# First matrix product of a fused block kernel: all eight chunks in plain fp32, small tables loaded later, norm rows sent later

## The chip, the cores and the metric

One Trainium2 chip, one core of it. The metric is device microseconds for one execution of the whole program. TensorE (PE) does the products, ScalarE (ACT) and VectorE (DVE) prepare operands and take results out of PSUM, GpSimd (POOL) helps, and SyncE (SP) issues nearly all DMAs.

## The reference, cut to what matters

The whole program computes three transformer-like blocks. The change touches only the opening of the first:

```
a0 = rmsnorm(h, norm_mix_pre[0])        # h: 272 tokens x 1024
a  = a0 @ w_dqkv                        # 1024 x (384 + 256 + 32)
c_q, c_kv, k_rope = split(a)            # c_q goes through a second rmsnorm ("cq")
```

The kernel multiplies h by the norm's gains, forms the product, and multiplies the outcome by one over the root mean square of each token afterwards. So the products don't wait for the norm; only what reads their results does.

## The kernel before, in words

Everything is kept transposed: 128 channels on the partitions, tokens along the free axis. h has eight chunks of 128 x 272. The weights come as a stream of units, and unit n uses slot n % 2 of three buffers: raw (as loaded), w_high (fp32r, the rounded part, made by ACT) and w_low (fp32r, the rest, made by DVE). The moving side is split in the same way into u_high (ACT) and u_low (DVE). A product of fp32 accuracy is then three fp32r products: high by high, high by low, low by high (the helper `three`, L519 to L521). The first units are dq (unit 0: 8 chunks x 3 blocks, for c_q), dkv (unit 1: 8 chunks x 2 blocks), dkr (unit 2: 8 chunks x 1 block), uqn (unit 3).

**The first unit is special.** Its weights go to the space of k_heads (`first_weights`) in four pieces of two chunks, each behind the two chunks of h that it meets (L382 to L385, semaphores h_in and pieces_in). Chunks 0 to 5 are multiplied as plain fp32: the stationary operand is the raw weight tile, the moving one is `first_u`, h times its gain (even chunks by ACT, L1376; odd ones by DVE, L1885). Each such product is two PE instructions in the profile, both at L812. Chunks 6 and 7 are done as `three`: ACT makes w_high of the last piece (L1385), DVE makes w_low (L1896), and only then does PE take them.

**The norm.** ACT squares each chunk into m (L1226), DVE adds the squares up in acc (L1890). Before chunk 6, PE waits for the parts of unit 0 and sums acc over the channels (`norm_sums`, L640, into bank 6). ACT takes the root (`rms`, L1243), DVE the reciprocal (L1699), and before chunk 7 PE spreads it over 128 partitions with the identity matrix (`norm_rows`, L672, into bank 7). DVE copies these rows out (`keep_rows`, L1732).

**The order of the work** is the program order of each engine, written out by hand; engines meet at semaphores. What matters around the change:

- SP: gains, the four pairs of pieces, ident (L386), dkv (L427), three small tables (par, rope, causal, L441); then dkr (L427) when the parts of unit 0 are made (`slot_free`), uqn when those of unit 1 are.
- ACT: for each piece the copy to first_u, two squares, two u_high (L1381); L1385; w_high of dkv's first half (L1205); the root (L1243); w_high of dkv's second half (L1208); a wait for the tables and ident; w_high of dkr (L1208); the squares of c_q (L1397); later the parts of uqn (L1415).
- DVE: for each piece first_u, two additions, two u_low (L1684); L1896; the reciprocal (L1699); w_low of dkv's first half (L1669); keep_rows (L1732); w_low of dkv's second half (L1675); c_q out of PSUM times the rows, three times (L1738); w_low of dkr (L1675); a wait for the tables; row_ident (L1929); the sum of c_q's squares (L1911, twice); further small steps.
- PE: chunks 0 to 5; the sums; chunk 6; the rows; chunk 7; then unit 1, whose first half needs DVE's L1669 and whose second half (chunk 4 on) needs all parts of unit 1. Before chunk 6 of unit 1 PE sums the squares of c_q (`latent_sums`, L820 and L822), for which it needs the second L1911; before chunk 7 it sends the rows of cq (L672).

Of the kernel before, what the change touches and what calls it, by code (L numbers as in the profile page):

```python
# [34 lines left out]
F32 = mybir.dt.float32  # L35
# [3 lines left out]
ALU = mybir.AluOpType  # L39
# [5 lines left out]
P = 128  # L45
D = 1024
DC = D // P
# [19 lines left out]
SCALE = float(NOPE + ROPE) ** -0.5  # L67
EPS = 1e-6

EPS_SHARE = EPS * D / P  # L70
WINDOWS = (2, 4, 8, 16)
GH, GDK, GDV = 4, 64, 128
# [21 lines left out]
FACTOR = -GUESS_A * 3.0 / 8.0  # L94


PIECES = DC // 2

# [126 lines left out]
def program(nc, dram, marks, final):  # L227
    ctx = ExitStack()
    with ctx:
# [21 lines left out]
        freed = {"v": sem("freed_v"), "a": sem("freed_a")}  # L251
        loaded = [sem("weights_loaded_0"), sem("weights_loaded_1")]
        tables_in, ident_in = sem("tables_in"), sem("ident_in")
        h_in = [sem(f"h_in_{c}") for c in range(PIECES)]
        pieces_in = [sem(f"first_unit_in_{c}") for c in range(PIECES - 1)]
        gains_in = sem("first_gains_in")
        p_in = sem("p_in")
        p_weights_in = sem("p_weights_in")
# [113 lines left out]

        def first_pieces():

            w = UNITS[0]["tiles"] * P // PIECES
            return [slice(p * w, (p + 1) * w) for p in range(PIECES)]


        @block.sync
        def _(sp):  # L380
            sp.dma_start(par[:, 0:DC], dram["par"][:, 0:DC]).then_inc(gains_in, 16)
            for p, cols in enumerate(first_pieces()):  # L382
                sp.dma_start(h[:, 2 * p:2 * p + 2, :], dram["h0"][:, 2 * p:2 * p + 2, :]).then_inc(h_in[p], 16)
                sp.dma_start(first_weights[:, cols], dram["w_dq"][0, :, cols])\
                    .then_inc(loaded[0] if p == PIECES - 1 else pieces_in[p], 16)  # L385
            sp.dma_start(ident[:, :], dram["ident"]).then_inc(ident_in, 16)  # L386

            def slot_free(n, shared=True):

# [17 lines left out]
            for name, units, tiles, _, _ in STREAM:  # L407
                n0, cols, src = FIRST_UNIT[name], tiles * P, dram["w_" + name]
                if units < 8:
                    for u in range(units):  # L410
                        n = n0 + u
                        if n == 0:
                            continue
                        if n >= 2:
                            slot_free(n, pool_share(n - 2))
                        if n == 2:
                            sp.wait_ge(loaded[0], 16)
                        dst, from_ = raw[n % 2][:, 0:cols], src[u, :, :]
                        if name == "dkr":

                            dst = dst.rearrange("p (k c) -> p k c", c=P)
                            from_ = from_.rearrange("p (k c) -> p k c", c=2 * P)[:, :, 64:64 + P]
                        if name == "uqr":

                            dst = dst.rearrange("p (k c) -> p k c", c=P)
                            from_ = from_.rearrange("p (k s c) -> p k s c", s=2, c=P)[:, :, 0, :]
                        sp.dma_start(dst, from_).then_inc(loaded[n % 2], 16)  # L427
                        if name == "uv":

                            sp.wait_ge(*done("k rope full"))  # L430
                            sp.dma_start(K[64:P, :, :], kr[64:P, :].unsqueeze(1).to_broadcast([64, NH, T1]))\
                                .then_inc(k_rope_in, 16)
                        if name == "uv":
                            q_rope_out(0)
                        if name == "wo" and u == 0:
                            for q4 in range(1, 4):
                                q_rope_out(q4)
                        if n == 1:
                            for dst, src_ in ((par[:, DC:NPAR], dram["par"][:, DC:NPAR]),
                                              (rope[:, :, :], dram["rope"]), (cmask[:, :], dram["cmask"])):  # L440
                                sp.dma_start(dst, src_).then_inc(tables_in, 16)  # L441
                else:

                    apart = 4 if pool_share(n0) != pool_share(n0 + 2) or not pool_share(n0 + 2) else 2 if not pool_share(n0 - 1) else 0
                    for u in range(apart):
                        slot_free(n0 + u, pool_share(n0 + u - 2))
                        sp.dma_start(raw[(n0 + u) % 2][:, 0:cols], src[u, :, :]).then_inc(loaded[(n0 + u) % 2], 16)
                    with sp.Fori(0, (units - apart) // 2) as i:
                        for k in range(apart, apart + 2):
                            n = 2 * i + (n0 + k)  # L450
                            slot_free(n, pool_share(n0 + k - 2))
                            sp.dma_start(raw[(n0 + k) % 2][:, 0:cols], src[2 * i + k, :, :])\
                                .then_inc(loaded[(n0 + k) % 2], 16)
# [45 lines left out]
        def _(pe):  # L499
# [292 lines left out]

            for k in range(DC):
                if k == DC - 2:
                    parts_ready(n)
                    norm_sums("a0", f"a0 acc {DC - 1}", squares(0, T1))
                if k >= DC - 2:
                    u_ready("a0")(k)
                else:
                    if k % 2 == 0:  # L800
                        pe.wait_ge(pieces_in[k // 2], 16)
                    pe.wait_ge(*done(f"a0 u {k}"))
                if k == DC - 1:
                    pe.wait_ge(ident_in, 16)
                    norm_rows("a0", token_rows(R_BANK, T1))
                for b in range(3):
                    out = bank[BLOCKS[b]["bank"]][:, 0:T1]
                    if k >= DC - 2:
                        last = three(out, *weights(n, 3 * k + b), uh[:, k, :], ul[:, k, :], False, k == DC - 1)
                    else:  # L810
                        tile = slice((3 * k + b) * P, (3 * k + b + 1) * P)
                        nc.tensor.matmul(out, first_weights[:, tile], first_u[:, k, :], start=k == 0, stop=False)  # L812
                    if k == DC - 1:
                        last.then_inc(products, 1)

            def latent_sums(name, j, what):
# [4 lines left out]
                for i, (t0, nt_) in enumerate(TILES):  # L821
                    last = nc.tensor.matmul(sums[0:nt_, i:i + 1], latent_sq[j][:, t0:t0 + nt_], over[:, what:what + 1],  # L822
                                            start=False, stop=True, skip_group_check=True)
                last.then_inc(*S.step(f"{name} sums"))
            unit(n + 1, T1, (uh, ul), u_ready("a0"), first_low="second unit low",
                 between={6: lambda: latent_sums("cq", 0, OVER_Q), 7: lambda: norm_rows("cq", latent_rows(R_BANK))})
            unit(n + 2, T1, (uh, ul))
            for k in range(QC):
                u_ready("c")(k)
# [361 lines left out]
        def _(act):  # L1191
# [177 lines left out]

            nc.scalar.activation(warm[:, :], ones[:, 0:1], ACT.Sqrt).then_inc(*S.step())  # L1370
            act.wait_ge(gains_in, 16)
            for p in range(PIECES):
                c = 2 * p
                act.wait_ge(h_in[p], 16)
                if p < PIECES - 1:
                    nc.scalar.activation(first_u[:, c, :], h[:, c, :], ACT.Copy, scale=pcol("mix_pre0", c))\  # L1376
                        .then_inc(*S.step(f"a0 u {c}"))
                for k in (c, c + 1):
                    square("a0", k, h[:, k, :], T1, S.step(f"a0 sq {k}"))
                for k in (c, c + 1):  # L1380
                    nc.scalar.activation(uh[:, k, :], h[:, k, :], ACT.Copy, scale=pcol("mix_pre0", k))\  # L1381
                        .then_inc(*S.step(f"a0 u high {k}"))
            cols = first_pieces()[PIECES - 1]
            act.wait_ge(loaded[0], 16)
            nc.scalar.activation(wh[0][:, cols], first_weights[:, cols], ACT.Copy).then_inc(high_parts, 1)  # L1385
            high(1, first="second unit", middle=lambda: rms("a0", 3))
            act.wait_ge(tables_in, 48)
            act.wait_ge(ident_in, 16)

            n = FIRST_UNIT["dq"]  # L1390
            high(n + 2)

            def latent_squares(js):
                for j in js:
# [265 lines left out]
        def _(dve):  # L1660
# [217 lines left out]
            nc.vector.memset(sq[:, :, :], 0.0).then_inc(*S.step())  # L1878
            nc.vector.memset(acc[:, :, :], EPS_SHARE).then_inc(*S.step("constants"))
            dve.wait_ge(gains_in, 16)  # L1880
            for p in range(PIECES):
                c = 2 * p + 1
                dve.wait_ge(h_in[p], 16)
                if p < PIECES - 1:
                    nc.vector.tensor_scalar(first_u[:, c, :], h[:, c, :], pcol("mix_pre0", c), None, ALU.mult)\  # L1885
                        .then_inc(*S.step(f"a0 u {c}"))
                for k in (c - 1, c):
                    dve.wait_ge(*done(f"a0 sq {k}"))
                    dve.wait_ge(*S.now())
                    nc.vector.tensor_tensor(acc[:, 0, 0:T1], acc[:, 0, 0:T1], m[:, k, :], ALU.add)\  # L1890
                        .then_inc(*S.step(f"a0 acc {k}"))
                for k in (c - 1, c):
                    u_low("a0", k, T1, 0, "mix_pre0")
            cols = first_pieces()[PIECES - 1]
            dve.wait_ge(high_parts, 1)
            nc.vector.tensor_tensor(wl[0][:, cols], first_weights[:, cols], wh[0][:, cols].bitcast(F32), ALU.subtract)\  # L1896
                .then_inc(low_parts_v, 1)
            norm("a0", tiles_of(T1))
            low(1, None, "second unit", lambda: keep_rows("a0", T1))

# [724 lines left out]
```

## Time and profile before

| | |
|---|---|
| median of 3 runs | 898.83 us (897.97 to 899.99) |
| profiled execution: span, first to last instruction | 896.4 us |
| profiled execution's own time | not listed apart from its span; the median lies 2.43 us above the span |
| PE busy | 882.7 us (98%) |
| DVE busy | 675.9 us (75%) |
| ACT busy | 503.2 us (56%) |
| POOL busy | 163.6 us (18%) |
| DMA | 146.81 MB, mean 164 GB/s |

The span runs from the first to the last instruction. Since PE is busy for nearly all of it, the page's shares tell little about a stretch of a few microseconds at the start; there the timeline of each engine is read beside that of the others. A row of the timeline has the start (us from the span's start), the duration, engine, line, operation, output and input, the count of instructions merged into it, and in brackets the idle time before it with what ended it. "SPq" is SyncE issuing a DMA.

### The profile page before, as it was taken

Reading aid. Unit: us, or ns where it says so; the run is one execution under the profiler, and the core shown is the slowest. Engines: PE = TensorE matmul, PEld = TensorE weight load, DVE = VectorE, ACT = ScalarE, POOL = GpSimd, SP = SyncE. Lnnn points to the kernel's source line nnn. Section 1 sums busy time; section 2 is a strip of 40 time slices with the busy share of each in tenths; the row PEclk is TensorE's granted clock in tenths of the full one; section 3 lists DMA queues with packets and bytes.
Section 4 is the critical chain, followed back from the end, with each engine's and each line's share of the span. In section 5 each row is a group of like instructions: output and inputs, shape, how many; then the busy total and the mean of one; then the engine's idle time right before and its main releaser. Section 6 shows DMA issues by size and latency. Waiting matters only on the chain.

```text
span 896.4 us, 19632 instructions
## 1 busy us (share of the span) xinstructions
PE 882.7 (98%) x7222; PEld 857.7 (96%) x7222; DVE 675.9 (75%) x1167; ACT 503.2 (56%) x853; POOL 163.6 (18%) x158
## 2 busy tenths in 40 slices
PE   9999999999999999999999999999999999999997
PEld 8977889999999998899999999999999999999997
DVE  7768459999994446999999544889888788875556
ACT  6777665666665347766666535554455444444443
POOL 0029530000001004200000003200032333313312
PEclk9999999999999999999999999999999999999999
DMA  7652134545455631354456454344434555564441
GB/s 251 197 126 88 58 132 158 177 181 187 167 213 184 236 152 47 107 189 182 180 187 223 168 204 158 118 166 141 141 142 171 196 188 185 186 229 176 170 141 48
DMA packets 25778, 146.81 MB, mean 164 GB/s; under 512 B 3040, under 2 KB 9216, under 8 KB 10496
## 3 DMA queue, kind: packets, MB, share of 16 engines
q1 hardware_dynamic: 25584, 145.99, 46.0%
q8 instruction: 33, 0.54, 0.3%
q14 instruction: 17, 0.14, 0.0%
q10 hardware_dynamic: 144, 0.13, 0.0%
HBM read 142.84 MB, written 1.05 MB: 161 GB/s over the span
## 4 chain that ended last, share of the span: by engine, by line
PE 94%; DVE 3%; ACT 1%; DMA 1%; issue 1%; POOL 0%; SPq 0%; DVEq 0%; POOLq 0%
PE bank L519 27%; PE bank L520 26%; PE bank L521 26%; PE bank L868 2%; PE bank L1091 1%; PE bank L884 1%; PE bank L657 1%; PE bank L672 1%; PE bank L902 1%; PE bank L640 1%; PE bank L812 1%; DMA k_heads<-w_dq_dram 1%; PE bank L1048 1%; PE bank L557 1%; PE bank L551 1%
## 5 line engine op out<-in xcount | busy, mean ns | idle before, releaser
L519 PE MATMUL bank<-u_high,w_high 128*128 128x256 f32 (+2 forms) x1318 | 376.6, 286 | 2.7 <-ACT u_high L1254 1.2
L520 PE MATMUL bank<-u_low,w_high 128*128 128x256 f32 (+2 forms) x1318 | 374.1, 284 | 0.0
L521 PE MATMUL bank<-u_high,w_low 128*128 128x256 f32 (+2 forms) x1318 | 373.0, 283 | 0.0
L519 PEld LDWEIGHTS bank<-u_high,w_high 128*128 128x128 f32 x1318 | 248.9, 189 | 5.7 <-ACT m L1226 1.7
L520 PEld LDWEIGHTS bank<-u_low,w_high 128*128 128x128 f32 x1318 | 248.6, 189 | 0.0
L521 PEld LDWEIGHTS bank<-u_high,w_low 128*128 128x128 f32 x1318 | 248.4, 188 | 0.0
L1675 DVE TENSOR_TENSOR w_low<-raw,w_high 128x1024 fp32r<-128x1024 f32 (+6 forms) x106 | 181.2, 1710 | 88.9 <-ACT w_high L1208 87.4
L1208 ACT ACTIVATE w_high<-raw 128x1024 fp32r<-128x1024 f32 (+6 forms) x115 | 179.9, 1565 | 66.8 <-PE bank L521 62.5
L519 PE MATMUL bank<-x_high,w_high 128*128 128x256 f32 (+1 forms) x592 | 167.9, 284 | 0.4 <-DVE x_low L2257 0.3
L521 PE MATMUL bank<-x_high,w_low 128*128 128x256 f32 (+1 forms) x592 | 168.2, 284 | 0.0
L520 PE MATMUL bank<-x_low,w_high 128*128 128x256 f32 (+1 forms) x592 | 167.3, 283 | 0.0
L2426 POOL TENSOR_TENSOR acc<-acc,sq 128x256 f32<-128x256 f32 (+1 forms) x32 | 44.2, 1382 | 496.4 <-ACT sq L1236 495.4
L519 PEld LDWEIGHTS bank<-x_high,w_high 128*128 128x128 f32 x592 | 111.7, 189 | 0.7 <-issue 0.7
L1205 ACT ACTIVATE w_high<-raw 128x1024 fp32r<-128x1024 f32 (+2 forms) x70 | 71.8, 1025 | 71.9 <-PE bank L521 69.7
L520 PEld LDWEIGHTS bank<-x_low,w_high 128*128 128x128 f32 x592 | 111.5, 188 | 0.0
L521 PEld LDWEIGHTS bank<-x_high,w_low 128*128 128x128 f32 x592 | 111.4, 188 | 0.0
L1669 DVE TENSOR_TENSOR w_low<-raw,w_high 128x1024 fp32r<-128x1024 f32 (+2 forms) x68 | 80.2, 1180 | 13.7 <-ACT w_high L1205 11.2
L1830 DVE SCALAR_TENSOR_TENSOR conv_out<-conv_in,par,conv_out 128x272 f32<-128x272 f32 (+1 forms) x176 | 78.9, 489 | 6.9 <-ACT conv_out L1288 1.4
L1738 DVE TENSOR_TENSOR conv_in<-bank,r_rows 128x256 f32<-128x256 f32 (+2 forms) x140 | 54.2, 427 | 16.0 <-PE bank L521 10.6
L2409 POOL TENSOR_TENSOR w_low<-raw,w_high 128x512 fp32r<-128x512 f32 (+1 forms) x22 | 46.0, 2089 | 85.9 <-ACT w_high L1208 85.9
L1295 ACT ACTIVATE conv_out<-conv_out 128x272 f32<-128x272 f32 (+1 forms) x44 | 18.7, 425 | 73.2 <-DVE conv_out L1830 73.2
L1236 ACT ACTIVATE sq<-bank 128x272 f32<-128x272 f32 (+1 forms) x24 | 9.4, 392 | 74.0 <-PE bank L521 72.1
(290 smaller groups left out, 1140.4 us busy)
## 6 DMA issues: line engine op xcount, KB each, us to landing
raw<-w_up_dram SPq DMA_DIRECT2D x66, 1024.0 KB, 4.8
raw<-w_down_dram SPq DMA_DIRECT2D x24, 1408.0 KB, 5.9
raw<-w_gin_c_dram SPq DMA_DIRECT2D x4, 1536.0 KB, 6.7
raw<-w_wo_dram SPq DMA_DIRECT2D x4, 1024.0 KB, 5.4
raw<-w_wout_dram SPq DMA_DIRECT2D x4, 1024.0 KB, 4.7
raw<-w_pgate_dram SPq DMA_DIRECT2D x4, 1024.0 KB, 4.8
raw<-w_gin_v_dram SPq DMA_DIRECT2D x2, 1024.0 KB, 4.7
raw<-w_gin_g_dram SPq DMA_DIRECT2D x2, 1024.0 KB, 5.5
```

The source lines that it names most:

```text
L519: nc.tensor.matmul(out, hi, rhi, start=start, stop=False)
L520: nc.tensor.matmul(out, hi, rlo, start=False, stop=False)
L521: return nc.tensor.matmul(out, lo, rhi, start=False, stop=stop)
L1205: nc.scalar.activation(wh[n % 2][:, 0:split], raw[n % 2][:, 0:split], ACT.Copy).then_inc(*S.step(first))
L1208: nc.scalar.activation(wh[n % 2][:, split:cols], raw[n % 2][:, split:cols], ACT.Copy).then_inc(high_parts, 1)
L1295: nc.scalar.activation(cv[:, 0, 0:T], cv[:, 0, 0:T], ACT.Silu).then_inc(*S.step(f"silu {l} {k}"))
L1669: nc.vector.tensor_tensor(wl[n % 2][:, 0:split], raw[n % 2][:, 0:split], wh[n % 2][:, 0:split].bitcast(F32), ALU.subtract)\
L1675: nc.vector.tensor_tensor(wl[n % 2][:, split:cols], raw[n % 2][:, split:cols], wh[n % 2][:, split:cols].bitcast(F32), ALU.subtract).then_i ...
L1738: nc.vector.tensor_tensor(out, bank[BLOCKS[b]["bank"]][:, 0:T], rows[:, 0:T], ALU.mult)\
L1830: nc.vector.scalar_tensor_tensor(cv[:, hf, 0:T], ur[:, hf, skip + tap:skip + tap + T], pcol(f"cw{l}", (tap * 2 + hf) * FC + j), cv[:, hf, ...
L2409: nc.gpsimd.tensor_tensor(wl[n % 2][:, at], raw[n % 2][:, at], wh[n % 2][:, at].bitcast(F32), ALU.subtract).then_inc(low_parts_g, pool_cou ...
L2426: nc.gpsimd.tensor_tensor(acc[:, a, 0:T], acc[:, a, 0:T], x, ALU.add).then_inc(*step)
```

## The change

It does four things. The list of pieces becomes a tuple of chunk pairs. Chunks 6 and 7 of unit 0 are multiplied as plain fp32 like the others: the split of the last piece's weights (L1385, L1896) is dropped, and the copies to first_u of chunks 6 (ACT) and 7 (DVE) come in. The norm's sums go from before chunk 6 to before chunk 7, its rows from before chunk 7 of unit 0 to before chunk 1 of unit 1. And SP issues ident after dkv, behind a new wait until dkv has landed, and the three tables behind ident; ACT's wait for the tables and ident goes behind its w_high of dkr.

```diff
+BY_SCALAR = (0, 2, 4, 6)
-PIECES = DC // 2
+PIECES = tuple((c, c + 1) for c in range(0, DC, 2))
...
         @block.sync
...
-                    .then_inc(loaded[0] if p == PIECES - 1 else pieces_in[p], 16)
-            sp.dma_start(ident[:, :], dram["ident"]).then_inc(ident_in, 16)
+                    .then_inc(loaded[0] if p == len(PIECES) - 1 else pieces_in[p], 16)
...
                         if n == 1:
+                            sp.wait_ge(loaded[1], 16)
+                            sp.dma_start(ident[:, :], dram["ident"]).then_inc(ident_in, 16)
                             for dst, src_ in ((par[:, DC:NPAR], dram["par"][:, DC:NPAR]),
                                               (rope[:, :, :], dram["rope"]), (cmask[:, :], dram["cmask"])):
                                 sp.dma_start(dst, src_).then_inc(tables_in, 16)
...
         @block.tensor
...
             for k in range(DC):
                 if k == DC - 2:
+                    pe.wait_ge(loaded[0], 16)
                     parts_ready(n)
-                    norm_sums("a0", f"a0 acc {DC - 1}", squares(0, T1))
-                if k >= DC - 2:
-                    u_ready("a0")(k)
-                else:
-                    if k % 2 == 0:
-                        pe.wait_ge(pieces_in[k // 2], 16)
+                for p, chunks in enumerate(PIECES[:-1]):
+                    if k == chunks[0]:
+                        pe.wait_ge(pieces_in[p], 16)
+                if k < DC - 2:
                     pe.wait_ge(*done(f"a0 u {k}"))
                 if k == DC - 1:
-                    pe.wait_ge(ident_in, 16)
-                    norm_rows("a0", token_rows(R_BANK, T1))
+                    norm_sums("a0", f"a0 acc {DC - 1}", squares(0, T1))
                 for b in range(3):
                     out = bank[BLOCKS[b]["bank"]][:, 0:T1]
-                    if k >= DC - 2:
-                        last = three(out, *weights(n, 3 * k + b), uh[:, k, :], ul[:, k, :], False, k == DC - 1)
-                    else:
-                        tile = slice((3 * k + b) * P, (3 * k + b + 1) * P)
-                        nc.tensor.matmul(out, first_weights[:, tile], first_u[:, k, :], start=k == 0, stop=False)
+                    tile = slice((3 * k + b) * P, (3 * k + b + 1) * P)
+                    last = nc.tensor.matmul(out, first_weights[:, tile], first_u[:, k, :], start=k == 0, stop=k == DC - 1)
...
+            def first_rows():
+                pe.wait_ge(ident_in, 16)
+                norm_rows("a0", token_rows(R_BANK, T1))
             unit(n + 1, T1, (uh, ul), u_ready("a0"), first_low="second unit low",
-                 between={6: lambda: latent_sums("cq", 0, OVER_Q), 7: lambda: norm_rows("cq", latent_rows(R_BANK))})
+                 between={1: first_rows, 6: lambda: latent_sums("cq", 0, OVER_Q), 7: lambda: norm_rows("cq", latent_rows(R_BANK))})
...
         @block.scalar
...
-                if p < PIECES - 1:
-                    nc.scalar.activation(first_u[:, c, :], h[:, c, :], ACT.Copy, scale=pcol("mix_pre0", c))\
-                        .then_inc(*S.step(f"a0 u {c}"))
+                for c in chunks:
+                    if c in BY_SCALAR:
+                        nc.scalar.activation(first_u[:, c, :], h[:, c, :], ACT.Copy, scale=pcol("mix_pre0", c))\
+                            .then_inc(*(S.step(f"a0 u {c}") if c < DC - 2 else (high_parts, 1)))
...
-            cols = first_pieces()[PIECES - 1]
-            act.wait_ge(loaded[0], 16)
-            nc.scalar.activation(wh[0][:, cols], first_weights[:, cols], ACT.Copy).then_inc(high_parts, 1)
             high(1, first="second unit", middle=lambda: rms("a0", 3))
+
+            n = FIRST_UNIT["dq"]
+            high(n + 2)
             act.wait_ge(tables_in, 48)
             act.wait_ge(ident_in, 16)
-
-            n = FIRST_UNIT["dq"]
-            high(n + 2)
...
         @block.vector
...
-                if p < PIECES - 1:
-                    nc.vector.tensor_scalar(first_u[:, c, :], h[:, c, :], pcol("mix_pre0", c), None, ALU.mult)\
-                        .then_inc(*S.step(f"a0 u {c}"))
+                for c in chunks:
+                    if c not in BY_SCALAR:
+                        nc.vector.tensor_scalar(first_u[:, c, :], h[:, c, :], pcol("mix_pre0", c), None, ALU.mult)\
+                            .then_inc(*(S.step(f"a0 u {c}") if c < DC - 2 else (low_parts_v, 1)))
...
-            cols = first_pieces()[PIECES - 1]
-            dve.wait_ge(high_parts, 1)
-            nc.vector.tensor_tensor(wl[0][:, cols], first_weights[:, cols], wh[0][:, cols].bitcast(F32), ALU.subtract)\
-                .then_inc(low_parts_v, 1)
             norm("a0", tiles_of(T1))
             low(1, None, "second unit", lambda: keep_rows("a0", T1))
```

## Rows read from the trace of the kernel before

**Rows 1.** The page, part 1: busy time, share of the span, instructions.
```profile
PE 882.7 (98%) x7222; PEld 857.7 (96%) x7222; DVE 675.9 (75%) x1167; ACT 503.2 (56%) x853; POOL 163.6 (18%) x158
```
**Rows 2.** PE's waits, whole span, longest total: us in total, times, longest.
```profile
PE bank L519 <- ACT u_high L1254: 1.2, 2, 1.0
```
**Rows 3.** The chain that ended last, in order of time: start, us, what.
```profile
8.41 5.77 PE bank L812 x24
14.18 0.49 issue
14.67 0.61 PE bank L640 x6
...
16.54 0.64 PE bank L672 x6
```
**Rows 4.** Timeline of PE around the norm's rows and unit 1.
```profile
16.38 0.80 PE L672 MATMUL bank<-ident,norm_y 91*128 91x91 f32 x6
...
18.18 0.29 PE L519 MATMUL bank<-u_high,w_high 128*128 128x272 f32 x1
...
22.71 0.35 PE L820 MATMUL bank<-ones,eps_weights 128*128 128x3 f32 x2
```
**Rows 5.** Timeline of ACT, 12 to 27 us.
```profile
12.43 0.83 ACT L1385 ACTIVATE w_high<-k_heads 128x768 fp32r<-128x768 f32 x1
14.47 1.06 ACT L1205 ACTIVATE w_high<-raw 128x1024 fp32r<-128x1024 f32 x1 [1.21 <-DMA raw<-w_dkv_dram]
15.43 0.15 ACT L1243 ACTIVATE norm_t<-bank 91x3 f32<-91x3 f32 x1
...
19.02 1.06 ACT L1208 ACTIVATE w_high<-raw 128x1024 fp32r<-128x1024 f32 x1 [2.48 <-DMA raw<-w_dkr_dram]
...
26.81 0.51 ACT L1415 ACTIVATE w_high<-raw 128x384 fp32r<-128x384 f32 x1
```
**Rows 6.** Timeline of DVE, 11 to 23 us.
```profile
11.89 0.99 DVE L1890 TENSOR_TENSOR acc<-acc,m 128x272 f32<-128x272 f32 x2
...
13.62 0.95 DVE L1896 TENSOR_TENSOR w_low<-k_heads,w_high 128x768 fp32r<-128x768 f32 x1
15.61 0.17 DVE L1699 RECIPROCAL norm_y<-norm_t 91x3 f32<-91x3 f32 x1 [1.04 <-ACT norm_t L1243]
15.71 1.19 DVE L1669 TENSOR_TENSOR w_low<-raw,w_high 128x1024 fp32r<-128x1024 f32 x1
17.21 0.44 DVE L1732 COPY r_rows<-bank 128x272 f32<-128x272 f32 x1 [0.32 <-PE bank L672]
17.69 1.22 DVE L1675 TENSOR_TENSOR w_low<-raw,w_high 128x1024 fp32r<-128x1024 f32 x1
18.83 1.13 DVE L1738 TENSOR_TENSOR m<-bank,r_rows 128x272 f32<-128x272 f32 x3
20.11 1.23 DVE L1675 TENSOR_TENSOR w_low<-raw,w_high 128x1024 fp32r<-128x1024 f32 x1
...
22.12 0.44 DVE L1911 TENSOR_TENSOR sq<-sq,m 128x272 f32<-128x272 f32 x1
```
**Rows 7.** Timeline of SP: DMA issues of the tables and of dkr.
```profile
5.01 0.65 SPq L386 DMA_DIRECT2D ident<-ident_dram  x1
...
7.65 0.47 SPq L441 DMA_DIRECT2D causal<-cmask_dram  x1
14.65 0.67 SPq L427 DMA_DIRECT2D raw<-w_dkr_dram  x1
```
**Rows 8.** DMA issues up to 60 us: count, KB each, median us to landing.
```profile
raw<-w_uqn_dram SPq DMA_DIRECT2D x1, 1536.0 KB, 6.9
...
raw<-w_dkr_dram SPq DMA_DIRECT2D x1, 512.0 KB, 4.2
...
ident<-ident_dram SPq DMA_DIRECT2D x1, 64.0 KB, 6.8
...
par<-par_dram SPq DMA_DIRECT2D x1, 4.0 KB, 1.7
```

More of the change, by code:

```diff
@@ L253, in program @@
         tables_in, ident_in = sem("tables_in"), sem("ident_in")
-        h_in = [sem(f"h_in_{c}") for c in range(PIECES)]
-        pieces_in = [sem(f"first_unit_in_{c}") for c in range(PIECES - 1)]
+        h_in = [sem(f"h_in_{c}") for c in range(len(PIECES))]
+        pieces_in = [sem(f"first_unit_in_{c}") for c in range(len(PIECES) - 1)]
         gains_in = sem("first_gains_in")
@@ L373, in first_pieces @@
         def first_pieces():
-            w = UNITS[0]["tiles"] * P // PIECES
-            return [slice(p * w, (p + 1) * w) for p in range(PIECES)]
+            w = UNITS[0]["tiles"] * P // DC
+            return [(slice(cs[0], cs[-1] + 1), slice(cs[0] * w, (cs[-1] + 1) * w)) for cs in PIECES]
         @block.sync
@@ L381, in _ @@
             sp.dma_start(par[:, 0:DC], dram["par"][:, 0:DC]).then_inc(gains_in, 16)
-            for p, cols in enumerate(first_pieces()):
-                sp.dma_start(h[:, 2 * p:2 * p + 2, :], dram["h0"][:, 2 * p:2 * p + 2, :]).then_inc(h_in[p], 16)
+            for p, (chunks, cols) in enumerate(first_pieces()):
+                sp.dma_start(h[:, chunks, :], dram["h0"][:, chunks, :]).then_inc(h_in[p], 16)
                 sp.dma_start(first_weights[:, cols], dram["w_dq"][0, :, cols])\
-                    .then_inc(loaded[0] if p == PIECES - 1 else pieces_in[p], 16)
-            sp.dma_start(ident[:, :], dram["ident"]).then_inc(ident_in, 16)
+                    .then_inc(loaded[0] if p == len(PIECES) - 1 else pieces_in[p], 16)
             def slot_free(n, shared=True):
@@ L1371, in _ @@
             act.wait_ge(gains_in, 16)
-            for p in range(PIECES):
-                c = 2 * p
+            for p, chunks in enumerate(PIECES):
                 act.wait_ge(h_in[p], 16)
-                if p < PIECES - 1:
-                    nc.scalar.activation(first_u[:, c, :], h[:, c, :], ACT.Copy, scale=pcol("mix_pre0", c))\
-                        .then_inc(*S.step(f"a0 u {c}"))
-                for k in (c, c + 1):
+                for c in chunks:
+                    if c in BY_SCALAR:
+                        nc.scalar.activation(first_u[:, c, :], h[:, c, :], ACT.Copy, scale=pcol("mix_pre0", c))\
+                            .then_inc(*(S.step(f"a0 u {c}") if c < DC - 2 else (high_parts, 1)))
+                for k in chunks:
                     square("a0", k, h[:, k, :], T1, S.step(f"a0 sq {k}"))
-                for k in (c, c + 1):
+                for k in chunks:
                     nc.scalar.activation(uh[:, k, :], h[:, k, :], ACT.Copy, scale=pcol("mix_pre0", k))\
                         .then_inc(*S.step(f"a0 u high {k}"))
-            cols = first_pieces()[PIECES - 1]
-            act.wait_ge(loaded[0], 16)
-            nc.scalar.activation(wh[0][:, cols], first_weights[:, cols], ACT.Copy).then_inc(high_parts, 1)
             high(1, first="second unit", middle=lambda: rms("a0", 3))
+            n = FIRST_UNIT["dq"]
+            high(n + 2)
             act.wait_ge(tables_in, 48)
             act.wait_ge(ident_in, 16)
-            n = FIRST_UNIT["dq"]
-            high(n + 2)
             def latent_squares(js):
@@ L1880, in _ @@
             dve.wait_ge(gains_in, 16)
-            for p in range(PIECES):
-                c = 2 * p + 1
+            for p, chunks in enumerate(PIECES):
                 dve.wait_ge(h_in[p], 16)
-                if p < PIECES - 1:
-                    nc.vector.tensor_scalar(first_u[:, c, :], h[:, c, :], pcol("mix_pre0", c), None, ALU.mult)\
-                        .then_inc(*S.step(f"a0 u {c}"))
-                for k in (c - 1, c):
+                for c in chunks:
+                    if c not in BY_SCALAR:
+                        nc.vector.tensor_scalar(first_u[:, c, :], h[:, c, :], pcol("mix_pre0", c), None, ALU.mult)\
+                            .then_inc(*(S.step(f"a0 u {c}") if c < DC - 2 else (low_parts_v, 1)))
+                for k in chunks:
                     dve.wait_ge(*done(f"a0 sq {k}"))
@@ L1891, in _ @@
                         .then_inc(*S.step(f"a0 acc {k}"))
-                for k in (c - 1, c):
+                for k in chunks:
                     u_low("a0", k, T1, 0, "mix_pre0")
-            cols = first_pieces()[PIECES - 1]
-            dve.wait_ge(high_parts, 1)
-            nc.vector.tensor_tensor(wl[0][:, cols], first_weights[:, cols], wh[0][:, cols].bitcast(F32), ALU.subtract)\
-                .then_inc(low_parts_v, 1)
             norm("a0", tiles_of(T1))
```

## Prediction

> **What bounds the kernel now.** I read the page first: PE is busy for 882.7 us of 896.4 [rows 1], so what counts is PE's order of work and its few gaps. Then the list of PE's waits: the largest entry is 1.2 us in total, and every entry is ended by an engine or by "issue", none by a DMA [rows 2]. So a delay at the start has nothing later to dissolve in: the transfers run ahead of PE, and what PE does wait for (DVE, ACT) works on PE's own results and shifts with it. Then the chain of waits around the edit: 24 passes of plain fp32 from 8.41 to 14.18, a gap of 0.49, the norm's sums (0.61), then chunk 6, the rows (0.64), chunk 7 [rows 3]; unit 1 begins at 18.18, and the sums of c_q's squares at 22.71 [rows 4]. Last the timelines of ACT, DVE and SP beside it [rows 5 to 7]. The thing to see is in DVE's: from 15.71 on it works almost without a break, and its last step before 22.71, the second L1911, ends at 22.12 + 0.44 = 22.56 [rows 6], while PE gets to the sums that need it at 22.71. DVE feeds PE with no slack worth the name at that point.
>
> **First unit, PE.** A plain product is two passes of 5.77 / 24 = 0.240 us [rows 3], 0.481 together. Three fp32r products take 3 x 0.126 = 0.378: 36 of them lie between 18.18 and 22.71 [rows 4]. Chunks 6 and 7 (six tiles) go from 6 x 0.378 = 2.27 to 6 x 0.481 = 2.89, so 0.62 more. The gap of 0.49 goes: it ends with DVE's w_low of the last piece (13.62 + 0.95 = 14.57 [rows 6]), which is no longer made. The rows leave this unit (-0.64) and return in unit 1 (+0.64). On paper PE is at 14.18 + 1.44 = 15.62 with chunk 6, 16.23 with the sums, 17.67 with chunk 7, and free of unit 0 half a microsecond earlier than 18.18.
>
> Here a rule speaks against the edit. The row shows 0.481 for an fp32 product [rows 3]. The Trainium skill, FP8 and Floating Point Precision, section TensorE Precision Notes, has true fp32 as four passes through the array. With the pass spacing of 0.126 that would be 0.504 as an estimate, so chunk 6 would end 0.07 later and everything behind it too. The measured 0.481 is used.
>
> **Covers of the first unit.** ACT's copy for chunk 6 and DVE's for chunk 7 come in, but L1385 (0.83) and L1896 (0.95) go [rows 5, 6]; both engines end no later. The last weight piece had landed by 12.43, when ACT read it without waiting [rows 5], and acc is complete at 11.89 + 0.99 = 12.88 [rows 6], about 13.4 with the added copies. PE needs them at 14.18 and 15.62: nothing. If this cover were gone, each microsecond of lateness would go straight to PE.
>
> **Unit 1, first half.** The sums now start at 15.62 instead of 14.67, 0.95 later. DVE takes the reciprocal before w_low of dkv's first half, in program order. Before, L1669 started at 15.71, 1.04 behind the start of the sums, and ended at 16.90 [rows 3, 6]. Now it ends at 15.62 + 2.23 = 17.85, and with 0.10 for the signal (14.57 to 14.67 in rows 3 and 6) PE starts unit 1 at 17.95, having waited 0.28. dkv itself is no limit: it came at 14.47 [rows 5], and with fewer transfers around it, no later.
>
> **The rows, and what is queued behind them.** This is the term that decides. PE sends the rows after chunk 0 of unit 1: 17.95 + 6 x 0.126 + 0.08 for the restart = 18.79, against 16.38 before [rows 4]. DVE's keep_rows followed 0.83 behind (17.21 [rows 6]), so now at 19.62, 2.41 later. Behind keep_rows DVE has, in this order: w_low of dkv's second half, c_q out of PSUM, w_low of dkr, row_ident, the two sums of squares. From 17.21 to 22.56 that is 5.35 us, and only 0.15 of it is idle (19.96 to 20.11, a wait for ACT's w_high of dkr) [rows 6]. So now it ends at 19.62 + 5.20 = 24.82, and PE can start the sums of cq at about 24.9. PE itself would be there at 17.95 + 0.08 + 36 x 0.126 + 0.64 = 23.2, so it stalls for 1.7 us before chunk 6 of unit 1. Chunk 4 is not held up: the second half of w_low is ready at 19.62 + 0.48 + 1.22 = 21.3, PE asks for it at 21.7. Against 22.71 PE is **2.2 us late** there. From there on the order of all engines is as before.
>
> **Tables, ident, dkr.** SP now waits for dkv to land (14.4 at the latest, from 14.47 in rows 5; perhaps 13.5, as 0.6 MB no longer share the engines), then issues ident and three tables, each 0.5 to 0.7 us [rows 7], then dkr. So dkr is issued at 16.1 to 17.0 instead of 14.65. It took 4.2 us [rows 8]; behind the tables perhaps half a microsecond more. It lands between 20.3 and 21.7, ACT has its w_high 1.1 later [rows 5], at 21.4 to 22.8. DVE comes to it at 22.3 (keep_rows at 19.62, plus 2.75 to the end of L1738 in rows 6). So 0 in the middle of the range, up to 0.5 at its end, more if the transfer is slower still. ident, issued about 14, needs between 1.7 (4 KB, empty queue) and 6.8 (behind all the weights) [rows 8]; I take near 2, as the queue is empty then. It is needed at 18.8, so nothing; at the far end it would add 2. The tables are read by DVE after 23.5. uqn is issued when w_low of unit 1 is done, now 21.4, takes 6.9 [rows 8] and lands at 28.3; ACT read it at 26.81 [rows 5], shifted to 29.0: 0.7 to spare. POOL only clears acc after the norm's sums, a microsecond later, and has nothing due; its queue isn't touched otherwise. ACT's wait for tables moves behind a wait (dkr) that ended later anyway.
>
> **The sum.** +2.2 on the profiled execution: 896.4 to 898.6 for the span. The median shown, 898.83, is 2.43 above that span; I carry this over: 901.0.
>
> **The rivals.**
> 1. dkr late. SP's wait puts dkr behind four issues. It decides once dkr lands after 21.2; each microsecond beyond goes to PE one for one, as low(dkr) stands before the squares in DVE's queue. A further microsecond, or ident near its far bound, gives 902.0. For it: dkr took 4.2 us for 512 KB in a quiet stretch, so it is a slow transfer. Against: the tables are nearly through when it starts.
> 2. Not slower: DVE's queue has room that the timeline hides. If the squares are there before PE at 23.2, that is, if what lies behind keep_rows can be done in 3.5 us and not in 5.2, only PE's own sum is left: 17.95 + 0.64 - 18.18 = +0.4, so 899.2. For it: a DVE late here could catch up if PE's later steps asked less of it, and a wait in the attention part could take some of it back. Against: the rows show no idle time to draw on, and PE's waits are short and none is for a DMA.
> 3. The edit does its plain job: PE free 0.5 us earlier and the rows slip into a hole. 898.3. For it: the gap of 0.49 does go. Against: 0.62 more product time, and PE has no hole in unit 1.
>
> **Chances.** Forecast (900.3 to 901.7) 0.58; rival 1 0.15; rival 2 0.20; rival 3 0.07. A measurement of this kernel can tell 0.2% from no change, 1.8 us: slower means above 900.6. A fifth of the forecast's own case lies below that (sums rounded my way, run spread of about 1 us), so slower 0.58 x 0.8 + 0.15 = 0.61, faster 0.04, same 0.35. Range 899.0 to 902.6: it leaves out rival 3 and the far tail of rival 1.
>
> **What would show it.** In the changed profile: L812-like passes without a gap from 8.41 to about 15.6, sums there, unit 1 from about 17.95, L672 at 18.8, keep_rows at 19.6, PE's L820 near 24.9 with an idle time of 1.5 to 1.9 us before it, released by DVE's L1911, and every stage from 25 us on shifted by about 2.2. Rival 1: ACT's w_high of dkr starts after 21.2 and DVE idles before its w_low. Rival 2: L820 at about 23.2. I am wrong if PE shows no wait before L820, or if the shift at 25 us isn't there at the end.

## The result, and the profile after

The changed kernel takes 901.37 us in the median of 5 runs (900.21 to 903.05), against 898.83 (897.83 to 899.99, 5 runs) before. The two medians are 2.5 us apart; the ratio is 1.0035, 95% interval 1.0024 to 1.0046, which is about 3.1 us slower. The spans of the two profiled executions, 899.5 and 896.4 us, are 3.1 us apart as well. The prediction said slower, by 2.2; the time lies in its range, but a good third of the loss came in a way that it did not have.

The changed profile, page part 1, and the longest entry of PE's waits:

```profile
PE 884.9 (98%) x7216; PEld 859.4 (96%) x7216; DVE 675.1 (75%) x1167; ACT 503.0 (56%) x853; POOL 163.6 (18%) x158
```
```profile
PE bank L818 <- DVE pool_gains L1925: 1.6, 1, 1.6
```

PE has one new wait, 1.65 us long (the list cuts it to 1.6), and it is now the longest of the program ([rows 2] had 1.2 in two). The timeline of PE shows where it is. Line numbers have moved: L810 is the plain fp32 product, L643 the norm's sums, L675 the rows, L818 and L820 the sums of c_q's squares.

```profile
15.34 0.57 PE L643 MATMUL bank<-mean_weights,acc 128*91 128x1 f32 x6
15.77 1.62 PE L810 MATMUL bank<-q_heads,k_heads 128*128 128x272 f32 x6
...
17.48 0.40 PE L522 MATMUL bank<-u_high,w_high 128*128 128x272 f32 x1
...
18.35 0.80 PE L675 MATMUL bank<-ident,norm_y 91*128 91x91 f32 x6
...
22.65 0.28 PE L524 MATMUL bank<-u_high,w_low 128*128 128x272 f32 x1
24.59 0.35 PE L818 MATMUL bank<-ones,eps_weights 128*128 128x3 f32 x2 [1.65 <-DVE pool_gains L1925]
24.80 0.72 PE L820 MATMUL bank<-mean_weights,sq 128*128 128x1 f32 x6
...
26.67 1.29 PE L675 MATMUL bank<-ident,norm_y 128*128 128x128 f32 x6
```

Unit 1 starts at 17.48, 0.7 earlier than before (18.18 in [rows 4]). Nearly all of that, 0.64 us, is the norm's rows, which PE has yet to send and now sends inside unit 1. Its last product before cq's sums starts at 22.65, so without the wait PE would have been at the sums at about 22.8, against 22.71 before: in PE's own work the edit gains nothing. The norm's rows are 2.0 later (18.35 against 16.38), and the sums of cq start at 24.59 instead of 22.71, **1.88 later**, behind 1.65 us in which PE does nothing. The releaser is named as DVE's pool_gains; it is the step beside the second sum of squares, which is what PE's wait asks for. DVE's timeline has the whole queue of [rows 6] again, shifted:

```profile
16.24 1.19 DVE L1667 TENSOR_TENSOR w_low<-raw,w_high 128x1024 fp32r<-128x1024 f32 x1
19.18 0.44 DVE L1730 COPY r_rows<-bank 128x272 f32<-128x272 f32 x1 [1.75 <-PE bank L675]
19.66 1.23 DVE L1673 TENSOR_TENSOR w_low<-raw,w_high 128x1024 fp32r<-128x1024 f32 x1
20.81 1.13 DVE L1736 TENSOR_TENSOR m<-bank,r_rows 128x272 f32<-128x272 f32 x3
21.99 1.23 DVE L1673 TENSOR_TENSOR w_low<-raw,w_high 128x1024 fp32r<-128x1024 f32 x1
...
24.00 0.44 DVE L1905 TENSOR_TENSOR sq<-sq,m 128x272 f32<-128x272 f32 x1
```

DVE stands idle for 1.75 us in front of keep_rows (0.32 before), and then needs 24.44 - 19.18 = 5.26 us to the end of the squares, as it did before (5.35). The second suspect, dkr, is close by. ACT's timeline, and SP's:

```profile
20.89 1.06 ACT L1209 ACTIVATE w_high<-raw 128x1024 fp32r<-128x1024 f32 x1 [3.83 <-DMA raw<-w_dkr_dram]
```
```profile
14.10 0.33 SPq L441 DMA_DIRECT2D ident<-ident_dram  x1
...
15.98 0.67 SPq L428 DMA_DIRECT2D raw<-w_dkr_dram  x1
```

dkr is issued 1.3 later and lands at 20.9 instead of 19.0. Its w_high ends at 21.95, and DVE begins w_low of dkr at 21.99, when it has just finished L1736 (21.94). Two limits end within 0.05 us of each other. The profile's chain that ended last goes through dkr here and has the late rows (18.35) nowhere:

```profile
15.98 4.88 DMA raw<-w_dkr_dram
20.89 1.07 ACT w_high L1209
```

A chain follows only the releaser that came last. Whether the other would have held as long has to be tried (runs 1 to 3).

The sums start 1.88 late, but the end is 3.1 late. The rest shows in the windows (busy time and count of PE, PEld, DVE, ACT, POOL; then granted clock as a share of 2.4 GHz, DMA share, GB/s), first after, then before:

```profile
20.00:25.00 5.00, 3.35 (x28) 3.16 (x27) 4.60 (x10) 2.02 (x4) 0.00 (x0) 1.00 0.60 189
25.00:30.00 5.00, 5.00 (x30) 4.96 (x30) 3.23 (x9) 1.55 (x5) 0.00 (x0) 0.66 0.88 289
26.00:27.00 1.00, 1.00 (x6) 1.00 (x6) 0.94 (x3) 0.00 (x0) 0.00 (x0) 0.50 0.89 326
30.00:35.00 5.00, 5.00 (x42) 5.00 (x41) 4.77 (x8) 5.00 (x9) 0.00 (x0) 1.00 0.01 2
```
```profile
25.00:30.00 5.00, 4.96 (x40) 4.77 (x39) 4.52 (x10) 3.95 (x7) 0.00 (x0) 1.00 0.50 136
```

From 25 to 30 us PE is busy throughout and gets 30 instructions done instead of 40: **the granted clock fell from 2.4 to 1.2 GHz** for some three microseconds behind the wait. The products there start 0.23 us apart (25.99 and 26.22) instead of 0.126:

```profile
25.99 0.43 PE L522 MATMUL bank<-u_high,w_high 128*128 128x272 f32 x1
26.22 0.43 PE L523 MATMUL bank<-u_low,w_high 128*128 128x272 f32 x1
```

What that costs shows in PE's next landmark, the first product of uqn, after and then before:

```profile
32.31 0.29 PE L522 MATMUL bank<-latent_high,w_high 128*128 128x272 f32 x1
```
```profile
29.08 0.36 PE L519 MATMUL bank<-latent_high,w_high 128*128 128x272 f32 x1
```

From the start of cq's sums to this product PE takes 7.72 us instead of 6.37, so the delay has grown from 1.88 to 3.23 there, and 3.1 is left of it at the end. So 3.1 = 1.88 (late squares) + 1.2 (lower clock). The Trainium skill (TensorE: Matmul & The Clock Gate, section HAM oscillation) says that idle gaps of PE bring the throttled clock back. The trace agrees in kind, 0.66 in the window behind the gap, but the page's rule speaks of longer gaps than the 1.65 us here; the measurement decides. What PE did before the clock fell: 1.65 us of nothing, then the short sums with one to three columns, then the first two products at full pace (25.45 and 25.68).

### The profile page after: what moved, and what is told of

It is laid out like the page before. It is cut to its first block, busy times and chain, and to the rows that moved or that the text cites. A ratio compares the mean times of both kernels' runs of the same rounds, so it can differ in the third digit from the quotient of the medians.

```text
span 899.5 us, 19618 instructions
## 1 busy us (share of the span) xinstructions
PE 884.9 (98%) x7216; PEld 859.4 (96%) x7216; DVE 675.1 (75%) x1167; ACT 503.0 (56%) x853; POOL 163.6 (18%) x158
## 3 DMA queue, kind: packets, MB, share of 16 engines
HBM read 142.84 MB, written 1.05 MB: 160 GB/s over the span
## 4 chain that ended last, share of the span: by engine, by line
PE 92%; DVE 3%; DMA 2%; ACT 1%; issue 1%; SPq 1%; POOL 0%; DVEq 0%; POOLq 0%
PE bank L522 26%; PE bank L523 26%; PE bank L524 26%; PE bank L869 2%; PE bank L1092 1%; DMA raw<-w_dkv_dram 1%; PE bank L885 1%; PE bank L660 1%; PE bank L675 1%; PE bank L903 1%; PE bank L643 1%; PE bank L1049 1%; PE bank L560 1%; PE bank L554 1%; PE bank L995 1%
## 5 line engine op out<-in xcount | busy, mean ns | idle before, releaser
L1736 DVE TENSOR_TENSOR conv_in<-bank,r_rows 128x256 f32<-128x256 f32 (+2 forms) x140 | 54.2, 427 | 16.1 <-PE bank L524 10.7
```

What stands on the lines that cost most here:

```text
L1736: nc.vector.tensor_tensor(out, bank[BLOCKS[b]["bank"]][:, 0:T], rows[:, 0:T], ALU.mult)\
```

## The experiments

Ten kernels ran, each timed in five rounds beside the kernel before on the same chip (its medians there 898.21 to 898.32 us). "Start of cq's sums" is 22.71 in the kernel before. The expectations name two theories of what holds DVE's queue: A, the late rows alone; B, the rows and dkr together.

**1. Rows right after unit 0.** The changed kernel with:

```diff
+            first_rows()
             unit(n + 1, T1, (uh, ul), u_ready("a0"), first_low="second unit low",
-                 between={1: first_rows, 6: ...
+                 between={6: ...
```

> The changed kernel, but the norm's rows are sent right after unit 0, ahead of the wait for unit 1, about 0.95 us earlier. Theory A (only the late rows delay DVE's queue): DVE is 0.9 earlier throughout, the sums of cq start at 23.7 instead of 24.6, the end is at least 0.9 us earlier. Theory B (dkr, issued behind ident and the tables, is a second limit that lies right behind the first: ACT's w_high of dkr started at 20.89 and DVE's w_low at 21.99): DVE's keep_rows comes 0.9 earlier but its w_low of dkr still starts at 22.0, the sums of cq stay at 24.6, and the time stays at +3 us over the kernel before.

Measured: 901.17 us, ratio 1.0033 (1.0020 to 1.0045): nothing gained. DVE and PE in its profile:

```profile
18.31 0.44 DVE L1731 COPY r_rows<-bank 128x272 f32<-128x272 f32 x1 [0.64 <-PE bank L675]
...
21.87 1.23 DVE L1674 TENSOR_TENSOR w_low<-raw,w_high 128x1024 fp32r<-128x1024 f32 x1 [0.81 <-ACT w_high L1210]
```
```profile
24.47 0.35 PE L818 MATMUL bank<-ones,eps_weights 128*128 128x3 f32 x2 [1.65 <-DVE pool_gains L1926]
```

keep_rows comes 0.9 earlier, and DVE loses it again in a wait of 0.81 for dkr's w_high, which wasn't there. That is theory B. The shown execution took 903.96 us, the other five 900.86 to 901.21; why it was longer is taken up at the end.

**2. Tables early, as before.** The changed kernel with:

```diff
+            sp.dma_start(ident[:, :], dram["ident"]).then_inc(ident_in, 16)
...
-                            sp.wait_ge(loaded[1], 16)
-                            sp.dma_start(ident[:, :], dram["ident"]).then_inc(ident_in, 16)
```

> The changed kernel, but SP issues ident ahead of dkv and the tables right behind dkv, without the wait, as before the change. Theory B (rows and dkr limit together): dkr's w_high is ready long before, but DVE still comes to w_low of dkr at 21.94 instead of 21.99, because the rows are as late; no change, +3 us. Rival (SP's order alone makes the loss): the sums of cq start 1 to 1.9 us earlier.

Measured: 901.28 us, ratio 1.0037 (1.0025 to 1.0049): nothing gained either. ACT has dkr's w_high at 17.17, nearly four microseconds earlier, and the sums of cq start at 24.12, 9.1 behind the norm's sums (15.02), as in the changed kernel (9.25). The rows now hold alone. ACT and PE in its profile:

```profile
17.17 1.06 ACT L1208 ACTIVATE w_high<-raw 128x1024 fp32r<-128x1024 f32 x1 [0.43 <-DMA raw<-w_dkr_dram]
```
```profile
24.12 0.36 PE L817 MATMUL bank<-ones,eps_weights 128*128 128x3 f32 x2 [1.52 <-DVE pool_gains L1924]
```

**3. Both.** (The first and the third run that the expectation names are runs 1 and 2 here.)

> The edits of the first and the third run of this call together: rows right after unit 0 and tables issued early. Theory B: only both together help. DVE comes to w_low of dkr at about 21.0, the sums of cq start at 23.5, PE waits some 0.8 us, the granted clock stays at 1.00, and the end is 0.8 us over the kernel before. Theory A: the same as the first run. If the clock falls here too, 2 us over.

Measured: 899.18 us, ratio 1.0012 (1.0003 to 1.0021), the start of cq's sums at 23.57:

```profile
23.57 0.35 PE L817 MATMUL bank<-ones,eps_weights 128*128 128x3 f32 x2 [0.74 <-DVE pool_gains L1925]
```

Each alone is worth nothing; together 2.0 of the 2.9 us by which run 1 lay above the same kernel before come back: 0.9 in DVE's queue (24.47 in run 1, 23.57 here), the rest with the clock, which stayed at 1.00 in this profile and fell in one execution of eleven. This is what two limits with the same end look like.

**4. DVE's order changed.** The changed kernel with c_q's squares added before the w_low of dkr:

```diff
             latents_in(range(QC))
+            add_latent_squares((1, 2))
             low(2)
+            norm("cq", 3)
...
-            add_latent_squares((1, 2))
...
-            norm("cq", 3)
```

> The changed kernel, but DVE adds c_q's squares before its w_low of dkr and takes cq's reciprocal right behind it. Theory: the stall is DVE's program order. The sums of cq then start near 23.7 (limited by ACT, which squares after its w_high of dkr), PE waits 0.8 us instead of 1.65, TensorE's granted clock stays at 1.00, and the end is 1.0 us over the kernel before instead of 3.1. Rival: the loss is in the fp32 products or in the DMA order, then nothing changes and it stays at +3.

Measured: 899.91 us, ratio 1.0018 (1.0009 to 1.0027), the sums at 23.27 behind a wait of 0.52.

```profile
23.27 0.35 PE L818 MATMUL bank<-ones,eps_weights 128*128 128x3 f32 x2 [0.52 <-DVE sq L1905]
...
30.18 0.36 PE L522 MATMUL bank<-latent_high,w_high 128*128 128x272 f32 x1 [0.58 <-DVE w_low L1948]
```

Rows, tables and products are as in the changed kernel; moving two additions, and cq's reciprocal behind them, takes 1.3 us off (against the 901.2 of runs 1 and 2). The sums came earlier than expected, and yet the end is 1.6 over the kernel before instead of 1.0. A wait of 0.58 for the first w_low of uqn comes up at 30.18, where the kernel before goes on almost without one: what DVE does earlier for one consumer it does later for the next.

**5. One part alone.** The kernel before, with nothing but the rows moved into unit 1.

> The kernel before with one part of the change: the norm's rows go from before chunk 7 of unit 0 to before chunk 1 of unit 1; products, tables and sums as before. Theory (the rows are the culprit): rows at 18.3, keep_rows at 19.1, the sums of cq at 24.4 to 24.5 instead of 22.7, PE waits 1.7 us there. With the clock falling behind that wait +3 us at the end, without it +1.7. Rival (it takes the fp32 products or the tables): within 0.5 us of the kernel before.

Measured: 899.99 us, ratio 1.0023 (1.0013 to 1.0033).

```profile
18.41 0.80 PE L672 MATMUL bank<-ident,norm_y 91*128 91x91 f32 x6
...
24.50 0.35 PE L817 MATMUL bank<-ones,eps_weights 128*128 128x3 f32 x2 [1.51 <-DVE pool_gains L1931]
```
```profile
25.00:30.00 5.00, 5.00 (x42) 4.96 (x42) 3.77 (x10) 2.33 (x6) 0.00 (x0) 1.00 0.90 297
```

The rows alone make the whole delay: 24.50, 1.79 late. In the profiled execution the clock stayed at 1.00 and the span is 898.1, 1.7 over the kernel before. The nine executions fall into two groups: five at a mean granted clock of 0.998 (899.63 to 899.99) and four at 0.996 or 0.997 (900.89 to 901.50). The same wait is followed by the fall in one execution and not in the next (by the mean clock, as only one execution has a profile), and the fall costs 1.3 us.

**6. The wait filled with work.** The changed kernel with eleven spare products in front of cq's sums:

```diff
             def latent_sums(name, j, what):
+                if name == "cq":
+                    for _ in range(11):
+                        nc.tensor.matmul(bank[5][:, 0:T1], wh[1][:, 0:P], uh[:, 0, :], start=True, stop=True)
                 pe.wait_ge(*done(f"latent squares {j}"))
```

> The changed kernel with 11 spare fp32r products of 128 x 272 (into a bank nobody reads) in front of the sums of cq, 1.4 us of work where PE waited 1.65. They compute nothing that is used. Theory C (the idle time makes the clock fall, and that costs 1.2 us on top): the sums still start at 24.6, the granted clock stays at 1.00 in 25 to 30, and the end is 1.2 us earlier than in the changed kernel, +1.9 over the kernel before. Rival (the clock is not tied to this gap): still 0.66 in 25 to 30 and +3.1.

Measured: 899.89 us, ratio 1.0018 (1.0009 to 1.0028); 0.998 or 0.999 in all eleven executions. The sums start at 24.68, no earlier than in the changed kernel, and PE is busy all along:

```profile
23.08 1.55 PE L818 MATMUL bank<-u_high,w_high 128*128 128x272 f32 x11
24.68 0.38 PE L821 MATMUL bank<-ones,eps_weights 128*128 128x3 f32 x2
```
```profile
25.00:30.00 5.00, 5.00 (x43) 4.96 (x43) 3.61 (x11) 2.13 (x6) 0.00 (x0) 1.00 0.94 311
```

Useless work in the gap makes the kernel about 1.5 us faster (1.0018 against 1.0035, each to the kernel before, timed beside it). From the sums to the first product of uqn PE takes 6.39 us again (24.68 to 31.07), where it took 7.72 with the fallen clock. That is the clock's part by itself. The changed kernel wasn't timed beside this one, but runs 5 and 7 were, and there the clock fell in 11 of 19 executions behind waits of 1.51 and 0.89 us; here it fell in none of 11. So the idle time was its cause.

**7 and 8. Dose.** The kernel before with three, and with one, useless copies on DVE ahead of the squares:

```diff
+            for _ in range(3):
+                dve.wait_ge(*S.now())
+                nc.vector.tensor_copy(xf[:, :], rows[:, :]).then_inc(*S.step())
             add_latent_squares((1, 2))
```

> The kernel before with three useless DVE copies (128 x 272, in a chain, 0.55 us each) ahead of the sums of c_q's squares. Theory: DVE has no slack there, so PE waits 1.6 us before the sums of cq, and nothing later takes it back: +1.6 at the end, and +2.8 if the clock falls behind the wait. Rival (later waits take it up): under +0.5.

> The same with one such copy, 0.55 us. Theory: PE waits 0.5 us, the granted clock stays at 1.00, +0.5 at the end: the clock part comes only with the long wait. Rival: the clock falls here too, +1.7. If later waits take it up: 0.

Measured: 900.33 us, ratio 1.0021 (1.0011 to 1.0030), and 898.81, ratio 1.0003 (0.9994 to 1.0012). A chained copy took 0.36 us, not 0.55 (the three 1.08, from 21.54 to 22.62), so the waits are 0.9 and 0.3:

```profile
23.76 0.35 PE L820 MATMUL bank<-ones,eps_weights 128*128 128x3 f32 x2 [0.89 <-DVE pool_gains L1934]
```
```profile
23.56 0.36 PE L820 MATMUL bank<-ones,eps_weights 128*128 128x3 f32 x2 [0.31 <-DVE pool_gains L1934]
```

With three copies the sums are 1.05 late and the profiled span, 897.3, is 0.9 over 896.4: nearly nothing of the delay is taken back later. With one copy the difference is within the noise, though its profile has the wait. In this second profile the norm's sums were themselves 0.4 late (15.11), so its 23.56 isn't the copy alone. With three copies, seven of ten executions ran at 0.996 or 0.997, with a median of 900.53, against 899.36 for the other three: again 1.2 us.

**9. Everything repaired.** Edits 1, 2 and 4 together.

> The changed kernel with rows right after unit 0, tables issued early, and DVE adding c_q's squares before its w_low of dkr (cq's reciprocal right behind it). Theory: no wait of PE before the sums of cq, which start at about 22.6; granted clock 1.00; the end within 0.3 us of the kernel before, rather below it. If the products in fp32 cost more than they look, up to +0.5.

Measured: 898.46 us against 898.32, ratio 1.0009 (0.9999 to 1.0019). The sums start at 22.54, 0.17 ahead of the kernel before, without a wait. It is lost at once: DVE is later for uqn.

```profile
29.37 0.36 PE L521 MATMUL bank<-latent_high,w_high 128*128 128x272 f32 x1 [0.58 <-DVE w_low L1948]
```

The kernel before restarts there at 29.08. One execution of the twelve took 903.48 at a mean clock of 0.997; what happened in it isn't known.

**10. The fp32 products alone.** The kernel before with chunks 6 and 7 in plain fp32, sums before chunk 6, rows before chunk 7, tables early.

> The kernel before with one part of the change: chunks 6 and 7 in plain fp32, the split of the last weight piece dropped; sums before chunk 6, rows before chunk 7, tables early, as before. Theory: 0.62 us more product time against the gap of 0.49 and what the first pieces give; unit 1 starts between 17.9 and 18.3 against 18.18, and the end is within 0.3 us of the kernel before. Rival (the fp32 products are a loss or a gain by themselves): more than 0.5 us either way.

Measured: 898.17 us against 898.32, ratio 0.9997 (0.9989 to 1.0006). The gap of 0.49 is gone and the longer products eat it.

```profile
14.57 0.57 PE L642 MATMUL bank<-mean_weights,acc 128*91 128x1 f32 x6
...
23.12 0.28 PE L819 MATMUL bank<-ones,eps_weights 128*128 128x3 f32 x2
```

From the end of chunk 5 to cq's sums it is 8.55 us (14.57 to 23.12), against 8.53 before (14.18 to 22.71). The expected start of unit 1 was missed in this profile (18.40), since PE was through chunk 5 and at the norm's sums only at 14.57, without a gap, where 14.18 had been taken. No version clearly beats the kernel before.

How often the clock fell, with PE's wait before cq's sums in each kernel's one profile:

| kernel | wait, us | executions with mean clock 0.997 or less |
|---|---|---|
| rows after unit 0 (1) | 1.65 | 6 of 6 |
| changed | 1.65 | 4 of 5 |
| tables early (2) | 1.52 | 6 of 6 |
| only rows moved (5) | 1.51 | 4 of 9 |
| three copies (7) | 0.89 | 7 of 10 |
| rows and tables (3) | 0.74 | 1 of 11 |
| squares first (4) | 0.52 | 0 of 11 |
| one copy (8) | 0.31 | 0 of 11 |
| wait filled (6) | none | 0 of 11 |
| everything repaired (9) | none (0.58 later, at 29.37) | 1 of 12 |
| fp32 products alone (10) | none | 0 of 11 |

## Why the prediction was right or wrong

**The deciding term held.** The prediction put the loss in DVE's queue behind keep_rows: 5.20 us from there to the end of the squares, 5.26 measured; PE 2.2 late at cq's sums behind a wait of 1.7, measured 1.88 and 1.65. Run 5 shows it with the rows alone, run 7 that there is no slack at the point: three copies of 1.08 us together made the sums 1.05 late.

**The first unit** came out earlier than its sum. The pass cost (0.240) was right, but the prediction took over the arrival at 14.18 from the profile of before, and with it two small losses that the changed execution did not have: a first product at 5.30 instead of 5.18, and some 0.2 us between the end of chunk 1 (12 passes from 5.30, so 8.18) and 8.41, where the second piece starts. The norm's sums started at 15.34, not 15.62. ACT, now idle, took the root 0.60 behind them and not 0.76. So unit 1 began at 17.48, not 17.95, without the wait of 0.28. That is more than the difference between 2.2 and 1.88. DVE gave 0.05 of it back at dkr, for which it was ready at 21.94 and which it began at 21.99.

**Tables and dkr**: issued at 15.98, 0.1 ahead of the forecast's 16.1 to 17.0; the transfer took 4.9 instead of 4.2, as it ran behind the tables; landing at 20.9 was within 20.3 to 21.7. ident landed 1.7 behind its issue, where about 2 had been taken. "Zero in the middle of the range" was right, but what it hid was that the two limits coincide: the prediction treated dkr as a rival with a surcharge, where it was a floor that made the other repair worthless (run 1).

**The step that failed is the sum "+2.2", which carries the delay at cq's sums to the end as it is.** The order of all engines did stay as before, as the prediction says, but the sum had no term for what 1.7 us of idle PE does to the clock. At the end PE was 3.1 late. The missing 1.2 us is the clock, shown by run 6 and by the two groups in runs 5 and 7. In the spans the miss is 0.9 (899.5 against 898.6): 1.2 too little for the clock, 0.3 too much for the delay at cq's sums. That the median, 901.37 against 901.0, comes so near is in part luck: the changed kernel's profiled execution lies 1.76 above its span (901.26), not the 2.43 that were carried over.

**The rivals.** Not slower (2): no room in DVE's queue, and PE's later waits took back next to nothing (3.23 late at 32.31, 3.1 at the end). The plain job (3): unit 1 did start earlier (17.48), but only because the rows had left unit 0; PE would have been at cq's sums at about 22.8 without its wait, no earlier than before, and run 10 shows that the gap gained is worth nothing once the fp32 products are paid. dkr late (1): true as a mechanism, but without a price of its own.

## What to carry to other kernels

When a result is sent later in one engine's order, cost what stands behind its reader in that reader's program order, not the reader alone: here one 0.44 us copy had 5 us of work behind it that PE needed without slack. Before repairing one cause of a delay, look whether another ends within a few hundredths of a microsecond of it; then only both repairs together show. And price a new wait of PE at more than its length: look at the granted clock of the window behind it, and if the wait can't be removed, spare products in it may be worth their place.

## What the runs showed of the hardware that was not expected

- A wait of PE of 1.65 us was followed by about three microseconds at 1.2 instead of 2.4 GHz, 1.2 us of loss. By the mean clock it happened also in most executions with 0.9 us (7 of 10), once in eleven with 0.74, and in none of eleven with 0.52. In the kernel before, with single waits of 1.0 us [rows 2] and 1.1 us (at its start) in other places, all 76 timed executions beside these runs had a mean clock of 0.998 or 0.999.
- It isn't a matter of the program alone: with one and the same kernel (run 5) the clock fell in four executions of nine. What decides between them stays open. In the profile of run 1 it stayed down longer, 0.51 from 25 to 30 us and still 0.81 from 30 to 35. From cq's sums to the first product of uqn PE took 9.16 us there (24.47 to 33.63) instead of 6.37, and that execution took 903.96 us.
